# Stick score banks handed back by a ScalarE copy, and two feature tiles moved into the attention of a two-block transformer kernel

## What is computed

```
h = rms_norm(x, norm_mix)
a_q, a_kv, a_g, b_qkv, c_qkv = split(h @ w_in)
o_a = nsa_mixer(a_q, a_kv, a_g)        # 4 heads: compressed, selected, window
o_b = dilated_mixer(b_qkv)             # 6 heads in 3 groups, merged
o_c = stick_breaking_mixer(c_qkv)      # 6 heads, strictly causal
x = x + concat(o_a, o_b, o_c) @ w_out
x = x + square(relu(rms_norm(x, norm_mlp) @ w_up)) @ w_down

# stick breaking, one block of 128 queries
z = q @ k.T * scale
log_beta, log_fail = log_sigmoid(z), where(causal, log_sigmoid(-z), 0)
after = reverse_cumsum(log_fail) - log_fail
a = where(causal, exp(log_beta + after), 0)
o = a @ v
```

## Time and profile before

| | |
|---|---|
| median of 3 runs | 1174.12 us (1172.09 to 1176.47) |
| the profiled execution | 1174.21 us, its span 1172.4 us |
| PE busy | 1114.2 us, 95% |
| weight loads on PE | 954.3 us, 81% |
| DVE, POOL, ACT busy | 641.7, 529.8, 424.9 us |
| chain that ended last | PE 76%, DVE 12%, ACT 5%, issue 4% |
| mean granted TensorE clock | 0.977 of full speed |

### The profile page before, as it was taken

How to read it: one execution, slowest core, us unless ns; L and a number is a source line. 1 busy time by engine, 2 the same in 40 slices (tenths; PEclk the granted TensorE clock), 3 DMA queues, 4 the chain that set the end, 5 groups by cost and what they waited for, 6 DMA issues and landing times.

```text
span 1172.4 us, 16124 instructions
## 1 busy us (share of the span) xinstructions
PE 1114.2 (95%) x5801; PEld 954.3 (81%) x5801; DVE 641.7 (55%) x1131; ACT 424.9 (36%) x852; POOL 529.8 (45%) x525
## 2 busy tenths in 40 slices
PE   6999999999989999999988987789999999999998
PEld 5788888888779888898888877788878888888887
DVE  6869777677567646485666586735641321321321
ACT  5373668363446532114553565423020110110110
POOL 0000000000443327989454177308976776777772
PEclk9999999999999999999999897699999999999999
DMA  6322322413211002323221000102322223223221
GB/s 249 125 88 90 110 88 93 141 54 126 90 54 37 20 18 73 126 90 127 72 73 55 18 2 18 55 1 91 125 91 97 101 90 108 90 93 104 89 89 54
DMA packets 27280, 97.18 MB, mean 83 GB/s; under 512 B 3024, under 2 KB 3408, under 8 KB 27088
## 3 DMA queue, kind: packets, MB, share of 16 engines
q1 hardware_dynamic: 27216, 96.32, 24.6%
HBM read 94.21 MB, written 2.10 MB: 82 GB/s over the span
## 4 chain that ended last, share of the span: by engine, by line
PE 76%; DVE 12%; ACT 5%; issue 4%; POOL 1%; DMA 1%; SPq 0%; DVEq 0%; POOLq 0%; ACTq 0%
PE bank L1236 21%; PE bank L1238 21%; PE bank L1237 21%; PE bank L788 4%; PE bank L751 3%; PE bank L768 3%; DVE arena L1967 1%; DVE wl L1918 1%; ACT wh L1597 1%; PE bank L810 1%; DVE arena L1021 1%; DMA x<-x_in 1%; POOL wl L1189 0%; DVE arena L2318 0%; DVE arena L939 0%
## 5 line engine op out<-in xcount | busy, mean ns | idle before, releaser
L1185 POOL TENSOR_TENSOR hold<-hold 128x2 f32<-128x2 f32 x117 | 29.3, 251 | 531.2 <-PE bank L1238 531.2
L1236 PE MATMUL bank<-xh,wh 128*128 128x512 f32 x568 | 226.5, 399 | 12.0 <-DVE xl L1887 9.4
L1237 PE MATMUL bank<-xl,wh 128*128 128x512 f32 x568 | 222.0, 391 | 0.0
L1238 PE MATMUL bank<-xh,wl 128*128 128x512 f32 x568 | 221.9, 391 | 0.0
L1236 PE MATMUL bank<-yh,wh 128*128 128x512 f32 x520 | 203.5, 391 | 2.0 <-DVE yl L2323 1.5
L1238 PE MATMUL bank<-yh,wl 128*128 128x512 f32 x520 | 202.6, 390 | 0.0
L1237 PE MATMUL bank<-yl,wh 128*128 128x512 f32 x520 | 202.5, 389 | 0.0
L1189 POOL TENSOR_TENSOR wl<-raw,wh 128x512 fp32r<-128x512 f32 x117 | 175.2, 1498 | 0.0
L1188 POOL TENSOR_TENSOR wl<-raw,wh 128x512 fp32r<-128x512 f32 x117 | 157.1, 1343 | 9.7
L1236 PEld LDWEIGHTS bank<-xh,wh 128*128 128x128 f32 x568 | 107.1, 189 | 35.1 <-issue 11.6
L1186 POOL TENSOR_SCALAR wh<-raw 128x1024 fp32r<-128x1024 f32 x117 | 126.6, 1082 | 0.0
(11 more groups left out here) (260 smaller groups left out, 1856.6 us busy)
## 6 DMA issues: line engine op xcount, KB each, us to landing
raw<-weight_units SPq DMA_DIRECT2D x173, 512.0 KB, 3.4
x<-x_in SPq DMA_DIRECT2D x4, 512.0 KB, 7.6
out_fm<-x SPq DMA_DIRECT2D x8, 256.0 KB, 2.0
arena<-tables SPq DMA_DIRECT2D x1, 1024.0 KB, 10.6
par<-params SPq DMA_DIRECT2D x1, 166.0 KB, 2.4
arena<-swa_table SPq DMA_DIRECT2D x1, 128.0 KB, 11.5
ident<-identity SPq DMA_DIRECT2D x1, 64.0 KB, 8.9
```

The costliest lines, as they stand in the source:

```text
L1185: pool.tensor_tensor(hold[:], hold[:], hold[:], ALU.add).then_inc(held, 1)
L1236: pe.matmul(out, lh, rh, start=start, stop=False)
L1237: pe.matmul(out, lh, rl, start=False, stop=False)
L1238: return pe.matmul(out, ll, rh, start=False, stop=stop)
```

## The change

1. ACT copies a stick group's scores from the bank to `pr` right behind `Abs`, and this copy hands the bank back. DVE's L1020 and L1025 then read the copy in place of the bank (in the changed file they are L1021 and L1024; what PE does at L751, L768, L788 and L810 is at L753, L770, L790 and L812 there). The wait for group i-4's transposes moves from DVE's difference to ACT's `Abs`; a new semaphore, `sdiff`, releases the last exponential.
2. Tiles 3 and 6 become pieces in two halves each, in groups 10 and 11, 12 and 13, in bank 7. Their units stand behind G1's. Their scaling on DVE, high halves on ACT and low halves on DVE become items of iterations 12 to 15.
3. The turn of the compressed keys comes in PE's iteration 0, their evacuation in ACT's iteration 1.
4. G1 lies in groups 1 to 8, G2 in 15 to 23, G3 in 26 to 35; the scales follow G2, in iterations 24 and 25. The twelve dilated turns lie in groups 35 to 53 (before, every second group from 28 to 50). Bank 7 joins the score banks at group 41 (before 36).

```diff
-U_F3 = U_F5 + 1
+U_G1 = U_F5 + 1
+U_F3 = U_G1 + 4
 U_F6 = U_F3 + 1
-U_G1 = U_F6 + 1
-U_G2 = U_G1 + 4
+U_G2 = U_F6 + 1
...
-TURNS2 = {28 + 2 * k: key for k, key in enumerate([("q", m) for m in range(6)] + [("k", m) for m in (0, 1, 2, 4, 5, 3)])}
-PIECE_STEPS = {"G1": (0, 1, 2, 3, 4, 5, 6, 7), "G2": (9, 12, 13, 14, 15, 16, 17, 18), "G3": (20, 23, 24, 25, 26, 27, 28, 29)}
+TURNS2 = dict(zip((35, 36, 38, 40, 41, 43, 45, 46, 48, 50, 51, 53),
+                  [("q", m) for m in range(6)] + [("k", m) for m in (0, 1, 2, 4, 5, 3)]))
+PIECE_STEPS = {"G1": (1, 2, 3, 4, 5, 6, 7, 8), "F3": (10, 11), "F6": (12, 13), "G2": (15, 17, 18, 19, 20, 21, 22, 23),
+               "G3": (26, 29, 30, 31, 32, 33, 34, 35)}
...
-WIDE_FROM = 36
-F6_HIGH, F6_LOW = 5, 6
+WIDE_FROM = 41
...
                         act.wait_ge(s["scores"], st + 1)
-                        if n3 >= 6:
-                            j = [j for j in range(i) if is_stick(j)][-2]
-                            act.wait_ge(*strip_read(groups[j]["strip0"]))
+                        if i >= 4:
+                            act.wait_ge(s["pt_ready"], groups[i - 4]["chunks"][-1][0] + 1)
 
                         act.activation(lt, score_bank(st)[:, 0:w], ACT.Abs).then_inc(s["soft1"], 1)
+                        act.activation(pr[:, 0:w], score_bank(st)[:, 0:w], ACT.Copy).then_inc(strip_read(st)[0], 1)
...
-                    act.wait_ge(*strip_read(g["strip0"]))
+                    act.wait_ge(s["sdiff"], stick_count(i) + 1)
...
-                    link(dve.scalar_tensor_tensor(out=lt, in0=z, scalar=0.0, in1=lt, op0=ALU.max, op1=ALU.add))
+                    link(dve.scalar_tensor_tensor(out=lt, in0=pr, scalar=0.0, in1=lt, op0=ALU.max, op1=ALU.add))
...
-                    if i >= 4:
-                        dve.wait_ge(s["pt_ready"], groups[i - 4]["chunks"][-1][0] + 1)
-                    dve.tensor_tensor(pr, z, lt, ALU.subtract).then_inc(strip_read(g["strip0"])[0], 1)
+                    dve.tensor_tensor(pr, pr, lt, ALU.subtract).then_inc(s["sdiff"], 1)
...
-            f_tile(3)
-            pe.wait_ge(heads_normed, 5)
-            free(("kcT", 0))
-            pe.transpose(B[BANK[("kcT", 0)]][:, 0:31], kcd[0:31, :], ident[0:31, 0:31]).then_inc(pe_misc, 1)
-
-            def behind_scores():
-                f_tile(6)
+
+            def turn_compressed():
+                pe.wait_ge(heads_normed, 5)
+                free(("kcT", 0))
+                pe.transpose(B[BANK[("kcT", 0)]][:, 0:31], kcd[0:31, :], ident[0:31, 0:31]).then_inc(pe_misc, 1)
```

More of the change, by code:

```diff
@@ L199, in plan @@
     seg2 += [("hid", 0, "A"), ("hid", 1, "A"), ("F", 4, "D")] + [("nT", j, "D") for j in range(6)]
-    seg2 += [("hT", 0, "A"), ("F", 2, "D"), ("kc", 0, "A"), ("F", 5, "D"), ("F", 3, "D"), ("kcT", 0, "A"), ("F", 6, "D")]
-    pieces = [(name, t) for name in PIECE_STEPS for t in range(TB)]
-    seg2 += [(name, t, "A") for name, t in pieces]
-    at2 = {key: 7 for key in [("F", 6)] + pieces}
+    seg2 += [("hT", 0, "A"), ("F", 2, "D"), ("kc", 0, "A"), ("F", 5, "D"), ("kcT", 0, "A")]
+    seg2 += [("G1", t, "A") for t in range(TB)] + [("F", 3, "D"), ("F", 6, "D")]
+    seg2 += [(name, t, "A") for name in ("G2", "G3") for t in range(TB)]
+    at2 = {item[:2]: 7 for item in seg2[-15:]}
+    at2["F", 5] = 5
     bank, free, before = {}, {}, {}
@@ L901, in act_part @@
                         soft1(i + LOOK)
-                    if a == 2 and i in TAKEN:
+                    if a == 2 and i == 1:
+                        behind_scores()
+                    if a == 2 and i in TAKEN and TAKEN[i][0][0] == "G":
                         item(TAKEN[i])
-                    if a == 2 and i == F6_HIGH:
-                        act.wait_ge(s["scores"], groups[7]["strip0"] + 1)
-                        item(("F", "high"))
+                    if a == 2 and i - 1 in TAKEN and TAKEN[i - 1][0][0] == "F":
+                        if TAKEN[i - 1][0] == "F6":
+                            act.wait_ge(s["scores"], groups[7]["strip0"] + 1)
+                        item(TAKEN[i - 1])
                     if a == 2 and i == SCALES_AT + 1:
@@ L1112, in dve_part @@
                         pair_out(pairs.index(i - OUT_LAG))
-                    if a == 2 and i in (-1, F6_LOW):
-                        item(("F", "scale" if i < 0 else "low"))
+                    if a == 2 and i in TAKEN and TAKEN[i][0][0] == "F":
+                        item((TAKEN[i][0], "scale"))
                     if 0 <= i + LOOK - 1 < ng:
```

41 lines of the change are left out of this document (21 added, 20 removed).

## The result

The changed kernel takes 1197.65 us (median of 4 runs, 1195.89 to 1199.52) against 1173.11 us (1171.89 to 1176.47) for the kernel before in the same series: ratio 1.0205, 95% interval 1.0175 to 1.0234, or 24 us. Ratios are taken over fast executions; the only other one of the whole series, 3869.79 us in the run with halved dilated operations, is in none. The profiled execution of it has a span of 1194.6 us and a mean granted clock of 0.967, against 1172.4 and 0.977. The forecast was 1175.0 with a range of 1164 to 1184; the measured time lies 22.7 us above it and 13.7 us above the range. PE's work is the same 5801 matmuls; the difference is time in which PE stood or ran at 1.2 GHz, and all of it lies inside the second attention: in the profiled executions the first matmul of the output projection comes at 803.73 us instead of 781.56, as much later as the whole span is longer.

The account below looks back on a forecast made before the run. TensorE (PE), at 95% of the span, was taken as the bound, with slack only inside the second attention. The terms 6.4 - 4.5 - 1.5 - 1.6 - 2.0 + 2.9 + 1.1 = +0.8 us gave 1175.0 us, range 1164 to 1184.

Parts of the forecast that it names:

- part 5: Stick groups from 35 on: DVE's two operations, now reading both inputs from SBUF, wait for busy POOL; +2.9 us, bounds 0 and +6.
- part 4: Stick groups' scores: ACT's copy costs 0, up to +2; earlier bank release gains 2.0 us, bounds -3 and 0.
- Part 2: Groups 10 to 13: feature tiles 3 and 6, as pieces, fill PE's idle time; -4.5 us, bounds -5 and -2.
- Part 1: Start of second attention: without tiles 3 and 6, the ACT and DVE chain stands bare; +6.4 us, bounds +2 and +9.
- Part 3: G2, G3 and key scales in later groups: -1.5 us (bounds -8 and +3), plus -1.6 from filling groups 29 to 35.
- the release does nothing: Stick groups' banks: ACT's copy comes no earlier than DVE's subtraction, the 2.0 us gain is missing; 1177 us, no chance given.
- Part 6: Dilated turns in groups 35 to 53: three more stand behind group 35, POOL just keeps up; +1.1 us, bounds +1 and +5.
- The slower rival: Dilated turns, groups 35 to 53: POOL and DVE block each other, POOL's cycle exceeds PE's 3.7 us; 1182 us, chance 0.23.
- list of what would show it: Signs in the second attention: some 8 us idle start, no group 12 wait, stalls at 24 to 28, no stick-bank waits.

## Why the prediction was wrong

**The step that failed most is part 5**, two operands from SBUF, forecast +2.9 us with bounds 0 and +6. With the copy and its early release (part 4, -2.0) it made +0.9; the run with these two alone gave +13.8 us (11.6 to 16.1). The mechanism was named. Its price per operation was about right where it was counted: in the eight groups from 35 on the 16 operations took 5.2 us more than before, 0.32 each, for 0.36 forecast; over all 48 it is 12.0 us, 0.25 each. Two factors were wrong. The count left out the scans, which the change does not touch and which took 5.2 us more, and the groups ahead of 35, of which five (0, 1, 9, 12, 22) took 9.6 us more: 5.8 us were forecast where DVE lost 17.2. And half of it was put on the path by DVE's busy share of 70%, where the measured time is 80% of what the trios lost. What a busy share cannot tell is that the trios stand in a chain that PE waits for. The Trainium skill, "SBUF — State Buffer", section "Who interferes with whom", which the forecast cited beside this term, was borne out: it calls the ports that DVE and GpSimd share an exclusive lock, and the rows at 756 to 762 us show both engines kept waiting for a whole instruction of the other. Its remark there that who is first, not the shape, decides who stands agrees too: the two-column operation took 194 ns or 1105 ns.

**Part 2** (tiles in groups 10 to 13, -4.5) is the term that failed in the first half of the order. Parts 1 and 2 make +1.9 together; the run with these, and G2 and G3 packed behind them, gave +5.2 (3.2 to 7.3). **Part 1** (+6.4) was read rightly: 5.5 us by the transpose of group 9, slow clock included, with the first piece 12.3 us behind tile 5 where 13.0 had been forecast. In the changed kernel it comes 15.3 us behind; that start costs 10.2 us because the copy's half falls into it too. So it was the -4.5 that did not come (unless the new places of G2 and G3 in that run hide it): it credited the whole of a gap's slack to work put into it.

**Part 3** (G2, G3, scales, -3.1 in its two terms) went to the other side: +5.4 beyond the turns, with an interval of about 4 us to either side. The forecast said that the scales' collision with a finish would be "the same DVE work beside less PE work" and still credited a gain; the waits of 4.71 and 2.48 us in the run with the late pieces show it in the new place. The fourth score bank moved in the same run and was not tested apart. The filling of groups 29 to 35 did come as forecast (PE is busy for all of 680 to 702).

**Part 4**: the copy's cost of 0 is shown in the new order, within the intervals. The bank release was given -2.0; in the old order no gain shows, as the rival "the release does nothing" had it. The waits for L1025 turned into waits for the next thing that DVE owes.

**Part 6** (turns, +1.1, bounds +1 and +5) measured +3.4 (1.3 to 5.4), inside its bounds. The slower rival's mechanism, a POOL cycle longer than PE's, did not occur: PE waited for POOL's doubling once, 1.9 us, as before. That rival had the right two engines in each other's way and the wrong one as victim.

The parts' effects as measured, 5.2 + 5.4 + 3.4 + 13.8 = 27.8 us, overshoot the whole, 24.0, by 4, which their intervals (2 to 4 us each) allow. Of the list of what would show it, the idle time in the start (7.9 us), the stall in groups 24 to 28 and operations above 0.69 us were found; the waits for stick banks vanished but for one of 3.48 us, on the copy. The wait of a compressed head's finish, off the list at group 12, had moved behind the pieces: 4.60 us (626.61), where it is 1.4 us without the copy. What stays open is why the order's second half costs what it does beyond the waits named, and how much of the 14 us that small POOL work gives the kernel before is the lock's.

## What to carry to other kernels

Before moving an operand of a VectorE instruction from a bank to SBUF, ask what GpSimd does meanwhile: in these runs such an instruction stood until a GpSimd instruction was over wherever GpSimd was busy, not only where VectorE looked full, and a row of dependent ones paid each time, an unchanged scan among them. A buffer freed early gave nothing where the engine that used to free it was the one waited for next. And work that covers a latency chain in front of a phase should be moved only into gaps whose own cause it removes: here its leaving cost 5.5 us, and the gaps that it went into gave next to nothing back.

## What the runs showed of the hardware

- A two-column POOL operation (128x2, read and write) takes 0.184 us at its least and 0.194 in the median, and up to 1.105 us when a two-operand DVE operation is under way.
- A chain of three DVE operations that each read two SBUF operands took 5.2 us at 512 columns (group 58 of the changed kernel) and 4.3 us at 384 (group 16) against POOL's splits, and 2.60 and 2.08 us with POOL idle. A single one at 128 columns rose from 0.29 to 1.1 us (group 9 with the copy in the old order).
- DVE's `TENSOR_SCALAR` from one SBUF operand to SBUF (L965) is not exempt: three of them ahead of the dilated groups took 3.08 us, 2.08 in the kernel before and 0.96 with POOL's work made small, and the longest single one 1.479 us where the median is 0.354. The first and third operations, where they read the bank, never rose above 0.69 us at 512 columns, neither in the kernel before nor in the changed one with the bank read.
- Operand space does not change the length by itself: L1024 at 128 columns took 0.29 us at its quickest from SBUF and L1025 0.29 us from the bank; at 512 columns both 0.69.
